# FF1's down product as seven block products, with its weight sums made in DRAM by adding transfers

## What is computed

```python
h2 = rms_norm(x, norm2_g[l])
up = h2 @ w_up[l].astype(h2.dtype)              # 1024 -> 2 * 2816
up = causal_depthwise_conv(up, ffn_dw_w[l])     # three taps
gate, val = jnp.split(up, 2, axis=-1)
x = x + (jax.nn.silu(gate) * val) @ w_down[l].astype(up.dtype)   # 2816 -> 1024
```

## Time and profile before

| | |
|---|---|
| Median of 3 runs | 2779.06 us (2777.92 to 2781.38) |
| The profiled execution, its own time | 2782.16 us |
| Its span, first to last instruction | 2780.5 us |
| PE busy | 2714.4 us, 98% of the span |
| DVE, ACT, POOL busy | 1758.4, 1131.0 and 640.6 us |
| FF1 up with its seven products | 582 to 939.9 us of the span |
| FF1 down | 939.9 to 1185 us |
| Granted TensorE clock, mean | 0.992 of full speed |

### The profile page before, as it was taken

How to read it: one execution, slowest core, us unless ns; L and a number is a source line. 1 busy time by engine, 2 the same in 40 slices (tenths; PEclk the granted TensorE clock), 3 DMA queues, 4 the chain that set the end, 5 groups by cost and what they waited for, 6 DMA issues and landing times.

```text
span 2780.5 us, 31459 instructions
## 1 busy us (share of the span) xinstructions
PE 2714.4 (98%) x12219; PEld 2197.0 (79%) x12219; DVE 1758.4 (63%) x2235; ACT 1131.0 (41%) x1590; POOL 640.6 (23%) x548
## 2 busy tenths in 40 slices
PE   9989999999999999999999999999999999999997
PEld 7877668788888788888878888766777888888886
DVE  6886554689999843243324444566548787776567
ACT  4423442343433443221235655665345322223543
POOL 1213111000110042010002222113423244444113
PEclk9999999999999999999999999999999999999999
DMA  3224532334444464344623232666543365657874
GB/s 123 84 83 140 145 80 103 140 104 122 130 121 121 157 234 138 117 150 157 214 84 102 69 99 85 173 183 189 195 169 125 137 213 188 204 189 248 262 251 133
DMA packets 147283, 414.45 MB, mean 149 GB/s; under 512 B 18616, under 2 KB 23352, under 8 KB 147136
## 3 DMA queue, kind: packets, MB, share of 16 engines
q1 hardware_dynamic: 115024, 309.97, 34.3%
q0 software_dynamic: 32112, 102.48, 11.9%
HBM read 309.46 MB, written 102.92 MB: 148 GB/s over the span
## 4 chain that ended last, share of the span: by engine, by line
PE 79%; DVE 12%; ACT 4%; issue 3%; DMA 2%; POOL 1%; SPq 0%; DVEq 0%; POOLq 0%; ACTq 0%
PE ps L218 77%; DVE cacc L189 3%; PE ps L221 2%; ACT PB L183 1%; POOL ga L186 1%; DVE cv L189 1%; DVE PB L189 1%; DVE tr L189 1%; DVE tl L186 0%; DVE YA L186 0%; DMA raw<-in_w_win 0%; DVE sqacc L186 0%; DVE ps L198 0%; DVE T L189 0%; DMA RBc<-scr_inv 0%
## 5 line engine op out<-in xcount | busy, mean ns | idle before, releaser
L218 PE MATMUL ps<-AH,wh 128*128 128x512 f32 (+1 forms) x1104 | 446.0, 404 | 19.4 <-DVE T L186 7.0
L218 PE MATMUL ps<-AH,wl 128*128 128x512 f32 (+1 forms) x1104 | 432.0, 391 | 0.0
L218 PE MATMUL ps<-AL,wh 128*128 128x512 f32 (+1 forms) x1104 | 431.6, 391 | 0.0
L218 PEld LDWEIGHTS ps<-AH,wh 128*128 128x128 f32 (+1 forms) x1104 | 206.6, 187 | 72.2 <-issue 10.4
L218 PE MATMUL ps<-stk,stk 128*128 128x512 f32 (+3 forms) x832 | 245.1, 409 | 12.8 <-DVE small L198 6.9
L218 PEld LDWEIGHTS ps<-AH,wl 128*128 128x128 f32 (+1 forms) x1104 | 206.5, 187 | 46.6
L218 PEld LDWEIGHTS ps<-AL,wh 128*128 128x128 f32 (+1 forms) x1104 | 207.0, 187 | 44.4 <-issue 2.9
L218 PEld LDWEIGHTS ps<-stk,stk 128*128 128x128 f32 x832 | 147.9, 191 | 83.2 <-issue 34.0
L186 DVE TENSOR_TENSOR wl<-raw,wh 128x1024 fp32r<-128x1024 f32 (+1 forms) x76 | 112.7, 1484 | 150.2 <-ACT wh L183 135.0
L218 PE MATMUL ps<-euh,ewt 128*128 128x512 f32 x640 | 198.8, 391 | 2.1 <-DVE eul L186 2.1
L186 POOL TENSOR_TENSOR wl<-raw,wh 128x1024 fp32r<-128x1024 f32 (+3 forms) x47 | 102.0, 2171 | 319.3 <-ACT wh L183 319.2
(11 more groups left out here) (324 smaller groups left out, 6373.6 us busy)
## 6 DMA issues: line engine op xcount, KB each, us to landing
ewr<-in_dn SPq DMA_DIRECT2D x88, 256.0 KB, 3.2
pwr<-in_w_up SPq DMA_DIRECT2D x38, 512.0 KB, 4.1
swr<-in_w_gu SPq DMA_DIRECT2D x38, 512.0 KB, 4.1
raw<-in_w_w2in SPq DMA_DIRECT2D x32, 512.0 KB, 4.2
scr_u<-cv SPq DMA_DIRECT2D x22, 512.0 KB, 2.6
eur<-scr_u SPq DMA_DIRECT2D x44, 256.0 KB, 3.4
scr_u<-uu SPq DMA_DIRECT2D x22, 512.0 KB, 8.6
alr<-in_dn POOLq DMA_DIRECT2D x11, 1024.0 KB, 9.9
```

The costliest lines, as they stand in the source:

```text
L218: return Issued(self, self.e.matmul(out, l, r, start=start, stop=stop, skip_group_check=onto))
```

## The change

- **FF1 down** has 7 passes of 11 steps (`DOWN1`), 77 steps of 12 matmuls, in place of 88. Each pass multiplies a block or a block sum of the weights (`s_s1`) by a block or a block sum of the activations (`s_t1`). Passes 2, 4 and 6 are added up in the banks of the passes two before them. The results go to the two token halves and the two channel halves as in `INTO1`. Every activation block is loaded anew (77 `u_load` in place of 44), and DVE makes all its low parts.
- **The weight sums** are made in the first stage: `weight_sums(x)` puts 88 transfers of 256 KB from DRAM to DRAM into POOL's list, four behind each `w_low(s)` from tile 4 on. There are eight phases of 11: copy, copy, add, add, copy, add, copy, add. Each phase from the third on waits until all transfers of the phases before it have landed.
- **The activation sums** are made by POOL during FF1 up: `block_sums(j)`, two loads of 512 KB, four TENSOR_TENSOR of 128x512 one after the other, one store of 1 MB. There is one for every two steps, behind the `added` of odd steps.
- **FF1 up** adds products up in PSUM. The seven products of a step use three banks, and the steps alternate between two sets of banks. One activation sum is negated so that only additions remain. DVE loses `shared`, `shared_end` and one of the additions of `value`; `value_end` becomes one multiplication of 512 columns, and `value_scaled` is one more. ACT copies three banks a step (`taken`, `taken_shared`, `taken_fifth`) in place of one, and PE's products 2, 4 and 5 wait for these copies, product 6 for DVE's `value`.
- The second and third quarter of the value weights come as blocks of their own (`value_load`), each as soon as its buffer is free.
- The last weight steps take other slots, and the first projection of the second block uses other banks.

```diff
 pool_a:
+        def weight_sums(x):
+            phase, k = divmod(x, NK)
+            a11, a21, a12, a22 = [self.io["dn1"][2 * k + i, h, :, :] for i in range(2) for h in range(2)]
+            s2, s3, s4, s1 = [self.io["s_s1"][i, k, :, :] for i in range(4)]
+            if phase > 1:
+                q.wait_ge(S.jd1, 16 * phase * NK)
+            if phase == 0:
+                q.dma(s1, a21).then_inc(S.jd1, 16)
+            elif phase == 1:
+                q.dma(s3, a11).then_inc(S.jd1, 16)
+            elif phase == 2:
+                q.dma_add(s1, a22, max_dma_last_dim=8192).then_inc(S.jd1, 16)
...
         for s in range(2, TILE["wout", 0] + 1):
             self.w_low(q, s)
             for n in after.get(s, ()):
                 spill(n)
+            for x in range(4 * (s - 4), min(4 * (s - 3), 8 * NK)):
+                if x >= 0:
+                    weight_sums(x)
 the products:
+    DOWN1 = [(("a", 0, 0), ("b", 0, 1)), (("a", 1, 0), ("b", 1, 1)), (("s", 0), ("t", 2)), (("s", 3), ("t", 1)),
+             (("s", 1), ("t", 0)), (("s", 2), ("b", 1, 0)), (("a", 1, 1), ("t", 3))]
+    INTO1 = [((0, 1, ALU.subtract),), ((0, 1, ALU.subtract),), ((0, 0, ALU.subtract),),
+             ((0, 0, ALU.add), (4, 0, ALU.subtract)), ((4, 0, ALU.add),), ((0, 0, ALU.subtract),), ((4, 1, ALU.add),)]
 pe_ff1:
-                if n == 0 and i == 4:
-                    q.wait_ge(S.uev, 6)
-                elif i == 0:
-                    q.wait_ge(S.ev1, 7 * (n - 1))
-                elif i == 1:
-                    q.wait_ge(S.snp1, n)
-                else:
-                    q.wait_ge(S.ev1, 7 * (n - 1) + (1, 2, 3, 4, 6)[i - 2] if n else 0)
+                if i == 0:
+                    q.wait_ge(S.uev, 2 * (PLAIN + n - 1) if n else 0)
+                elif i == 2:
+                    q.wait_ge(S.snp1, 3 * n + 1)
+                elif i == 4:
+                    q.wait_ge(S.snp1, 3 * n + 2)
+                elif i == 5:
+                    q.wait_ge(S.snp1, 3 * n + 3)
+                elif i == 6:
+                    q.wait_ge(S.ev1, 3 * n + 2)
                 part(n, i)
-        for w in range(88):
-            p, k = w // 22, w % 22
+        for w in range(7 * NK):
+            p, k = w // NK, w % NK
             q.wait_ge(S.dwl1, w + 1)
-            q.wait_ge(S.dul1, 22 * (p // 2) + k + 1)
+            q.wait_ge(S.dul1, w + 1)
 dve_ff1, the last step of FF1 up and what follows:
             else:
                 d_low(0)
                 u_low(0)
+                d_low(1)
             value(n)
+            value_scaled(n)
             if more:
                 s_lows(n + 1, 3)
             else:
-                d_low(1)
+                u_low(1)
+                d_low(2)
+            gate_end(n)
         value_end(NQ - 1)
-        u_low(1)
+        u_low(2)
         taps(0, NFF - 1)
-        d_low(2)
-        u_low(2)
 pool_ff1:
+        def block_sums(j):
+            q.wait_ge(S.tl1, 4)
+            q.wait_ge(S.jd1, self.SUMS1_END + 16 * j)
+            q.wait_ge(S.du1, 32 * j + 32)
+            for x in range(2):
+                q.dma(self.TW1[:, 2 * x:2 * x + 2, :], self.io["s_u1"][2 * j + x, :, :]...
+            b12, b11, b22, b21 = [self.TW1[:, x, :] for x in range(4)]
+            q.wait_ge(S.jl1, 32 * j + 32)
+            q.tt(b11, b12, b11, ALU.subtract).then_inc(S.jb1)
+            q.wait_ge(S.jb1, 4 * j + 1)
...
+            q.dma(self.io["s_t1"][j, :, :, :], self.TW1[:, :, :]).then_inc(S.jd1, 16)
+        added(0)
+        for n in range(1, NQ):
             added(n)
-        q.wait_ge(S.dul1, 10)
-        for u in range(10, 22):
-            u_low(u)
+            if n % 2:
+                block_sums(n // 2)
```

More of the change, by code:

```diff
@@ L395, in __init__ @@
             self.EU_FREE.append(free)
+        for x in range(2):
+            one = Area(nc, sq + 4096 * x, sq + 4096 * x + 4096)
+            self.EUR.append(Area(nc, one.lo + 2048, one.hi).get("eur", [P, 512])[:, :])
+            self.EU.append(tuple(one.get("eu", [P, 512], F32R)[:, :] for _ in range(2)))
+            self.EU_FREE.append(7)
+        self.TW1 = Area(nc, sq, sq + 8192).get("tw1", [P, 4, 512])
         w = Area(nc, lo + 4096, TOP)
@@ L1760, in act_ff1 @@
+            taken_shared(n)
+            if n + 1 < NQ:
+                high(n + 1, 4)
+            else:
+                d_high(0)
+                u_high(0)
+            taken_fifth(n)
+            if n + 1 < NQ:
+                high(n + 1, 5)
+                high(n + 1, 2)
+            else:
+                for w in range(1, 4):
                     d_high(w)
                     u_high(w)
-            tap_gate(PLAIN + n)
+        tap_gate(NFF - 1)
+        tap_value(NFF - 1)
         d_high(4)
@@ L1786, in square @@
             else:
[L1787 to L1803 removed]
+                for x in range(m):
+                    if x % 2 == m % 2 and x not in (0, 4):
+                        q.wait_ge(*self.added1(x))
@@ L1804, in act_ff1 @@
+                q.act(self.sqF[m % 2][:, :], self.XR[:, n, c], ACT.Square).then_inc(self.squared1(m)[0])
+        for w in range(6, 7 * NK):
+            d_high(w)
+            u_high(w)
+            if 52 <= w < 56:
+                square(w - 52)
+            if 63 <= w < 67:
+                square(4 + w - 63)
+                into(0, 4 + w - 63)
+            if 72 <= w < 76:
+                square(8 + w - 72)
+                into(0, w - 72)
         for n in range(4):
@@ L2159, in sp_ff1 @@
         u_load(9)
-        for w in range(9, 88):
+        for w in range(9, 7 * NK):
             d_load(w)
-            if w < 21:
+            if w < 7 * NK - 1:
                 u_load(w + 1)
@@ L2186, in ready @@
         def ready(k):
-            q.wait_ge(S.pl, 8 * half + k + 1)
+            q.wait_ge(S.pl, 8 + k + 1 if half else (k + 4) % 8 + 1)
         def norm(half, k):
```

364 lines of the change are left out of this document (198 added, 166 removed), and 4 rows, old and new, of the table SHARED.

## The result

The changed kernel takes 2790.05 us (median of 11 runs, 2782.79 to 2796.72), the kernel before 2781.01 us beside it on the same chip (11 runs, 2774.20 to 2784.28). The ratio is 1.0034, 95% interval 1.0024 to 1.0044: 9 us slower, where 25 us less were forecast, and outside the range. The profiled execution of the changed kernel has an own time of 2788.33 us and a span of 2786.2.

The account below looks back on a forecast made before the run. PE, busy 98% of the span, was taken as the bound. The terms -29.9 - 3.9 + 6.4 + 2.0 = -25.4 us, from the median of 2779.06 us, gave 2754 us, range 2749 to 2758.

Parts of the forecast that it names:

- the two terms: FF1 down: 132 matmuls removed, -29.9 us; at its start, waits and half clock mostly gone, -3.9 us (0 to -4.7).
- rival 5: FF1 down: two loads a step starve PE, so products do not become fewer in effect; 2779 us or so, chance 0.02.
- POOL's list in the first stage: First stage: adding transfers delay POOL's `w_low` and so PE; +6.4 us, between 0 and 17.
- The delays at tile 10 I cost at nothing: First stage, tile 10: PE waits 7.04 us for DVE anyway; without that cover about 3.5 us.
- I take 1.0 for this and the two other boundaries: First stage, near 231.83 us and two nearby boundaries: only 1.0 us lost, since PE is by then late itself.
- the wait near 183 us: First stage, tile 13: PE waits 3.7 us for `w_low(13)`, behind an adding transfer's landing taken as 5.2 us.
- the event at half clock, 1.65 us: First stage: an idle PE is followed by one stretch at half clock, costing 1.65 us.
- FF1 up, POOL against DVE: FF1 up: POOL's four `block_sums` instructions every second step slow DVE, one or two misses; +2.0 us, bounds 0 and 32.
- ACT's copies at nothing: FF1 up: ACT's two more bank copies a step, each with 2.7 us before PE needs it, cost nothing.
- Rivals 1 and 2: First: POOL's list stalls PE in the first stage, 10 to 17 us, 0.20; second: FF1 up's port, 10 to 32, 0.13.
- Rival 4: First stage: adding transfers within DRAM land late, beyond 13 us, making the kernel slower than before; chance 0.05.
- the remaining edits I cost at nothing: Value weights loaded by block, other slots at the end, other banks in the first projection: nothing, at most 4 us once.

Follow-up runs that it names:

- no sums: The changed kernel without the 88 weight-sum transfers, FF1 down reading other data: 2768.80 us, ratio 0.9955 to the kernel before.
- last fit: The changed kernel with transfers moved to six attention heads and the output projection, and orders and loads changed: 2769.56 us, ratio 0.9953 to the kernel before.

## Why the prediction was wrong

**What bounds the kernel, FF1 down, its start: right.** 924 matmuls, no half clock at its start; 33.3 us less in the profile where the two terms gave 33.8. One wait of 1.4 us, at 1001.5 us, was above the 1 us that was said. Nothing else starved PE, rival 5 fell.

**POOL's list in the first stage: the step that failed**, with +6.4 us forecast, 17 as bound, and 22 measured (no sums). Four things in it:
- "The delays at tile 10 I cost at nothing" failed. The cover was real in the kernel before, but it was DVE that PE waited for, and DVE shared the delay: PE waited 5.8 us for POOL and then still 4.8 for DVE, 3.6 more than the 7.04 of before.
- "I take 1.0 for this and the two other boundaries": the waits for landings there were 7.0 and 11.1 us, not 5.2. A phase ends behind eleven transfers or more, and they don't land as one alone: the four issued from 248.1 to 249.7 us took 11.3 to 14.7.
- The issue was taken as 1.08 us from the records of `pwr`. Records of issues overlap: at tile 13 three issues held the list for 1.54 us, not 3.2. What grew was the low part behind them, 3.20 us in place of 2.40, which the sum had at its old length. The two errors nearly cancel: that the wait near 183 us measured 3.1 where 3.7 were forecast is in part luck.
- That the issues slow DVE stood nowhere in the sum. Taps: +7.6 us in the changed kernel, +12.9 once the waits were gone. It was argued from the earlier trace rows for POOL's low parts, and not carried to POOL's issues, of which there were 88, nor to low parts made longer by them.

Of the event at half clock, 1.65 us, nothing can be said: over the first 340 us the mean granted clock was 0.97 before, 0.96 in the changed kernel, and 0.96 without the sums, where the program of the stage is the old one.

**FF1 up, POOL against DVE: the second term that failed**, +2.0 forecast, 12.5 in the profile; POOL's additions alone are worth 10.6 us. The room of 3.4 us before `value` was worked out with DVE's instructions at their length without POOL. I had weighed the rule of the Trainium skill (SBUF — State Buffer, "SBUF: two separate sides") by FF2 up and chosen against it; it gave 16 us. The measured 10.6 us lies between my 2.0 and those 16, nearer to the rule; for each addition VectorE lost 0.8 us of the 1.76 that it took, not its length. FF2 up was the wrong witness: PE at 100% there says that DVE had room, not that the two don't collide.

**ACT's copies at nothing: failed at both ends**, 2.5 us in step 0 and 1.2 in step 1, and 3.0 in place of 0.8 in the last step. "The longest such piece is a rounding of 1024 columns" left out that a rounding can itself wait for a load (5.42 us). In the steps between it held.

**The rivals.** Rivals 1 and 2 both came true at once, above the first one's price (22 for 10 to 17) and at the foot of the second's (12.5 for 10 to 32). I had given them 0.20 and 0.13 as if one excluded the other, and their sum of 34 us, more than the gain, was no case of its own. (The times written for rival 1 are 1 to 2 us above what its 10 to 17 us give.) Rival 4 named the right place but the wrong lever: no landing of 13 us was needed, since waits for landings were only a third of the price in front, and FF1 up had a price of its own.

**What stays open.** Of the 3.3 us behind FF1 down, 1.6 are a wait at the start of the second block's first projection, which begins 1.8 us after FF1 down's last matmul, where the kernel before has 0.23:

```profile
1188.83 0.47 PE L218 MATMUL ps<-AH,wh 128*128 128x512 f32 x1 [1.42 <-issue]
```

All seventeen kernels with the new FF1 down have this wait (1.0 to 1.5 us idle), and the one before hasn't, so it belongs to the change; "the remaining edits I cost at nothing" failed here. The trace names no releaser, and the new banks of that projection weren't tried apart. The other 1.7 us, with one more stretch at 1.2 GHz, may be chance: kernels whose orders differ only in front show 1596.7 to 1602.9 us for that part. How the issues slow VectorE's instructions and POOL's low parts stays open too; no run here separates writing descriptors from POOL's other work in an issue.

## What to carry to other kernels

A stall that is covered by another wait is only free if the other engine doesn't share the delay; before costing it at nothing, ask what that engine is waiting for. In one list per engine, a wait for a landing is paid by the next thing in the list that somebody needs, and moving it moves the bill: put it where nothing urgent stands behind it, and put enough work between the issue and the wait (in the last fit 21 to 23 us from the first of eleven issues to the wait left no wait). POOL's work beside a full VectorE has a price even when POOL itself has plenty of idle time, and that holds for issuing transfers as for arithmetic.

## What the runs showed of the hardware

- An adding transfer between two DRAM tensors held POOL's list for 0.52 us, a plain copy for 0.49. The adding one's record ran on beside the next instruction: 0.76 us at the least, 1.35 in the middle, up to 3.39, four together 3.2. 256 KB landed 6.7 us after the issue in the middle (2.7 to 14.7), a sixteenth of it 3.6 (1.8 to 7.9).
- A low part of 128x1024 on POOL right behind four adding issues took 3.6 us, behind copies 2.4.
- With such transfers in POOL's list VectorE's instructions with three SBUF operands were longer: 1688 to 1728 ns in the mean without them, 1839 with copies, 1971 with adding transfers, 2046 with thin adding ones.
- A POOL addition of 128x512 and VectorE's instructions beside it both grow: 1.29 to 1.76 us for the one, 0.8 us of VectorE's time for each of them.
